# Putting the experts' sums back to the tokens with rounded parts of 512 columns in place of plain float32 products

## The chip, the cores and the metric

The kernel runs on one core of a Trainium2 chip. The core has TensorE (matrix products into the accumulator banks, PSUM), VectorE, ScalarE, GpSimd, and a sync engine (SyncE) that issues the large transfers from device memory; 16 DMA engines carry them. The engines run apart and wait for one another only by semaphores. The metric is the time of one execution on the device in microseconds, the median of several runs. All numbers are float32; a "rounded" tile (float32r in the trace) is a float32 tile that TensorE reads in a shortened form, in one pass instead of several.

## What is computed

The reference runs one block of four sublayers and then a second block of two layers over 256 tokens of 1024 channels. The change lies in the last sublayer of the first block, a mixture of eight experts with two chosen per token:

```python
def moe_ffn(h, router, w_gu, w_down):
    logits = (h @ router).astype(jnp.float32)
    top_val, top_idx = lax.top_k(logits, TOP_K)
    weights = jax.nn.softmax(top_val, axis=-1)
    gate = jnp.sum(jax.nn.one_hot(top_idx, N_EXPERTS, dtype=jnp.float32) * weights[..., None], axis=-2)
    out = jnp.zeros(h.shape, jnp.float32)
    for e in range(N_EXPERTS):
        out = out + gate[..., e:e + 1] * swiglu(h, w_gu[e], w_down[e])
    return out
```

With `swiglu(h, w_gu, w_down)` the product of silu(g) * u with `w_down`, where g and u are the two halves of `h @ w_gu`. Each expert is 1024 x 7168 and 3584 x 1024, 44 MB of weights.

## The kernel before

**One expert at a time, for the tokens it has.** The kernel first works out which tokens each expert takes (up to 128 fit in one round; a second round, called `again`, runs only if some expert has more, and is skipped here by a branch on a flag (`second`, L2755, with the test at L190 and the skipped side's semaphore counts at L195)). For an expert x a one-hot matrix `Pe` (tokens by places) gathers its tokens by a product into `XGf` and its rounded parts `XGh`, `XGl`. Then 14 weight tiles of 512 columns give seven pairs of rows (`hrow`), which are turned and split into `hTh`, `hTl`, and 28 row blocks of the second matrix give the sum of 128 places by 1024 channels in two accumulator banks.

**Products in three parts.** To keep float32 accuracy, every weight and every activation is split into a rounded high part and the rest: high times high, high times low and low times high are accumulated. Weights arrive in slots of 2 MB (three of them, `slots`), and each slot is used in two *units* of 128 x 2048. For every unit ScalarE copies the slot into `uh_moe_w` (rounding, `split_hi`, L362), VectorE subtracts (`ul_moe_w`, `split_lo`, L374), and TensorE does twelve products of 512 columns. An expert has 42 units, numbered l = 0 to 41 below: 0 to 27 for the first matrix, 28 to 41 for the second. High and low parts have three buffers each, so the high part of unit n waits until TensorE has used unit n-3 (L368). A slot is given back when the low part of its second unit is done (L380).

**The end of an expert and the put.** When the sum is complete, `summed_vector` (L2635) multiplies it by the sublayer's gate row into `Y`, two pieces of 512 columns (the tile shows as `HT` in the trace, since Y lies in it). `put_tensor` (L2531) then brings it back to the tokens: for each half `hf` of the tokens and each half `i` of the channels one product with `PT`, the turned one-hot matrix, as weights and a piece of Y streamed through:

```python
e.matmul(ps.t[:, :], PT[x % 2][:, hf, :], Y[:, i * 512:(i + 1) * 512])
```

`put_vector` (L2540) adds the four results, times the token's gate, to X.

**What sets the order.** Nothing is scheduled by a planner: each engine's stream is written by the loops `round_tensor`, `round_scalar` and `round_vector` (L2649 to L2678). ScalarE and VectorE run two units ahead: at step n they split unit n and then do `use_scalar` or `use_vector` of unit n-2. So on VectorE the sums of expert x (`use_vector`, l = 41) stand behind the low part of unit 1 of expert x+1 and ahead of that of unit 2. On TensorE the put of expert x stands behind unit 3 of expert x+1, in the middle of its weight products. For the last expert it stands at the end: the sums, the put, the additions, and then the norm that begins on ScalarE (`norm_scalar`, L526, after a table load, L142). On VectorE the last sums and the additions stand behind the branch (`last_put`, L2829); on ScalarE the branch comes after the last unit's high part. The second block's first layer starts with memsets on GpSimd, which wait for TensorE's count behind its own branch, and then the first splits (`uh_in`, `ul_in`).

Of the kernel before, what the change touches and what calls it, by code (L numbers as in the profile page):

```python
# [6 lines left out]
F32 = mybir.dt.float32  # L7
R32 = mybir.dt.float32r
AF = mybir.ActivationFunctionType
AX = mybir.AxisListType  # L10

D = 1024
# [11 lines left out]
NE = 8  # L24
# [1008 lines left out]
def hybrid(c):  # L1033
# [586 lines left out]
    def branch_tensor(e, br):  # L1620
# [3 lines left out]
        for hf in range(2):  # L1624
# [22 lines left out]
            e.wait_ge(*ps.was)  # L1647
            e.wait_ge(*v.at(("PT", br, hf)))
            e.wait_ge(*a.at(("PT", br, hf)))
# [729 lines left out]
def experts(c):  # L2379
# [5 lines left out]
    M = c.moe = Stage(c, "moe")  # L2385
    again = c.again = Stage(c, "again")
    HT = c.put(98.5, "HT3", [128, KC, T])
    ph = c.above(114.5)
    PT = [c.sb(f"PTe{i}", [128, 2, 128], ph) for i in range(2)]
    rw = c.sb("rw", [128, KC, NE], ph)  # L2390
    L, gt = c.sb("L", [128, 2, NE], ph), c.sb("egate", [128, 2, NE], ph)
    sel, pos = c.sb("esel", [128, 2, NE], ph), c.sb("epos", [128, 2, NE], ph)
# [5 lines left out]
    hTh, hTl = c.put(40.5, "ehTh", [128, 28, 128], R32), c.put(54.5, "ehTl", [128, 28, 128], R32)  # L2398
    XGh, XGl = c.put(106.5, "XGh", [128, KC, 128], R32), c.put(110.5, "XGl", [128, KC, 128], R32)
    XGf, Y = HT[:, 0:4, :].rearrange("p a (b s) -> p (a b) s", s=128), HT[:, 4:8, :].rearrange("p a b -> p (a b)")  # L2400
    Pe = c.put(68.5, "Pe", [128, 2, 128])
    hrow = [c.put(70.5 + 2 * i, f"hrow{i}", [128, 512]) for i in range(2)]
    router_landed, norm_landed, raw_landed = c.event_signal("router_landed", 16), c.event_signal("final_norm_landed", 16), c.event_signal("raw_landed", 16)
# [21 lines left out]
    NU, PER = len(U), 42  # L2425
    dbanks, ubanks = c.pool(range(6, 8)), c.pool(range(6))

    def at(n):

        return n // PER, n % PER  # L2430
# [35 lines left out]
    def gather_vector(e, S, blk, x, step):  # L2466
        if step == 0:
            e.wait_ge(*M.v.at("pos"))
            if x:
                e.wait_ge(*S.t.at(("XG", x - 1, 4)))  # L2470
            for hf in range(2):
                e.tensor_scalar(Pe[:, hf, :], K["iota"][:, blk * CAP:blk * CAP + 128], pos[:, hf, x:x + 1], ALU.is_equal, sel[:, hf, x:x + 1], ALU.mult).then_inc(*S.v.up(("Pe", x)))
        if step == 2:
            ps = c.psum.of((S.name, "PT", x))
            e.wait_ge(*S.t.at(("PT", x)))
            if x > 1:
                e.wait_ge(*S.t.at(("put", x - 2)))
            e.tensor_copy(PT[x % 2][:, :, :].rearrange("p h t -> p (h t)"), ps.t[:, 0:256]).then_inc(*S.v.up(("PT", x)))
            c.psum.leave((S.name, "PT", x), S.v)
        if step in (3, 4):  # L2480
            k0 = 4 * (step - 3)
            ps = c.psum.of((S.name, "XG", x, k0))
            e.wait_ge(*S.t.at(("XG", x, k0)))
            if x:
                e.wait_ge(*S.v.at(("XGl", x - 1, 4)))
            else:
                e.wait_ge(*M.t.at("logits"))
            for k in range(k0, k0 + 4):
                e.tensor_scalar(XGf[:, k, :], ps.t[:, (k - k0) * 128:(k - k0 + 1) * 128], s1[:, k:k + 1], ALU.mult, s2[:, k:k + 1], ALU.add).then_inc(*S.v.up(("XGf", x, k0)))
            c.psum.leave((S.name, "XG", x, k0), S.v)  # L2490
        if step == 5:
            for k0 in (0, 4):
                e.wait_ge(*S.a.at(("XGh", x, k0)))
                e.tensor_tensor(XGl[:, k0:k0 + 4, :], XGf[:, k0:k0 + 4, :], XGh[:, k0:k0 + 4, :].bitcast(F32), ALU.subtract).then_inc(*S.v.up(("XGl", x, k0)))
# [19 lines left out]
    def hidden_scalar(e, S, x, j):  # L2514
        ps = c.psum.of((S.name, "hT", x, j))
        e.wait_ge(*S.t.at(("hT", x, j)))
        if x:
            e.wait_ge(*S.t.at(("Y", x - 1, 1)))
        elif S is M:
            e.wait_ge(*S.v.at(("w", "lo", 7)))  # L2520
        e.activation(hTh[:, 4 * j:4 * j + 4, :].rearrange("p a s -> p (a s)"), ps.t[:, :], AF.Copy).then_inc(*S.a.up(("hTh", x, j)))
# [9 lines left out]
    def put_tensor(e, S, x):  # L2531
        for hf in range(2):
            for i in range(2):
                ps = ubanks.take((S.name, "put", x, hf, i))
                e.wait_ge(*ps.was)
                e.wait_ge(*S.v.at(("Y", x, i)))
                e.matmul(ps.t[:, :], PT[x % 2][:, hf, :], Y[:, i * 512:(i + 1) * 512]).then_inc(*S.t.up(("put", x, hf, i)))
        S.t.mark(("put", x))

    def put_vector(e, S, x):  # L2540
        e.wait_ge(*M.v.at("gate"))
        for hf in range(2):
            for i in range(2):
                o = X[:, hf, i * 512:(i + 1) * 512]
                ps = c.psum.of((S.name, "put", x, hf, i))
                e.wait_ge(*S.t.at(("put", x, hf, i)))
                if x:
                    e.wait_ge(*S.v.at(("X", x - 1)))
                e.scalar_tensor_tensor(o, ps.t[:, :], gt[:, hf, x:x + 1], o, ALU.mult, ALU.add).then_inc(*S.v.up(("X", x)))
                c.psum.leave((S.name, "put", x, hf, i), S.v)  # L2550
            if x == NE - 1:
                S.v.mark(("X_half", hf))
# [44 lines left out]
    def use_scalar(e, S, n):  # L2597
        x, l = at(n)
        if l < 28:
            j = l // 4  # L2600
            if l % 4 == 1 and j:
                hidden_scalar(e, S, x, j - 1)
            if l % 4 == 3:
                ps = c.psum.of((S.name, "row", x, j, 0))
                e.wait_ge(*S.t.at(("row", x, j, 0)))
                if j > 1:
                    e.wait_ge(*S.t.at(("hT", x, j - 2)))
                elif x:
                    e.wait_ge(*S.t.at(("hT", x - 1, 6 - j % 2)))
                e.activation(hrow[j % 2][:, :], ps.t[:, :], AF.Silu).then_inc(*S.a.up(("silu", x, j)))  # L2610
                c.psum.leave((S.name, "row", x, j, 0), S.a)
        elif l == 28:
            hidden_scalar(e, S, x, 6)

    def use_vector(e, S, n):
        x, l = at(n)
        if l < 28:
            j = l // 4
            if l % 4 == 1 and j:
                hidden_vector(e, S, x, j - 1)  # L2620
            if l % 4 == 3:
                ps = c.psum.of((S.name, "row", x, j, 1))
                e.wait_ge(*S.t.at(("row", x, j, 1)))
                e.wait_ge(*S.a.at(("silu", x, j)))
                e.tensor_tensor(hrow[j % 2][:, :], hrow[j % 2][:, :], ps.t[:, :], ALU.mult).then_inc(*S.v.up(("h", x, j)))
                c.psum.leave((S.name, "row", x, j, 1), S.v)
            if l == 3 and x:
                put_vector(e, S, x - 1)
            return
        if l == 28:  # L2630
            hidden_vector(e, S, x, 6)
        if l == PER - 1 and (x < NE - 1 or S is again):
            summed_vector(e, S, x)

    def summed_vector(e, S, x):  # L2635
        e.wait_ge(*c.side.v.at(("gate", "moe")))
        e.wait_ge(*(S.t.at(("put", x - 1)) if x else M.t.at("logits")))
        for i in range(2):
            ps = c.psum.of((S.name, "Y", x, i))
            e.wait_ge(*S.t.at(("Y", x, i)))  # L2640
            e.tensor_tensor(Y[:, i * 512:(i + 1) * 512], ps.t[:, :], g[:, i * 512:(i + 1) * 512], ALU.mult).then_inc(*S.v.up(("Y", x, i)))
            c.psum.leave((S.name, "Y", x, i), S.v)
# [26 lines left out]
    def round_vector(e, S, W, blk, begun):  # L2669
        for n in range(NU + AHEAD):  # L2670
            if (EARLY if S is M else 0) <= n < NU:
                W.split_lo(e, n)
            if n == AHEAD - 1:
                begun(e)
            if n >= AHEAD:
                use_vector(e, S, n - AHEAD)
                if coming(n - AHEAD):
                    gather_vector(e, S, blk, *coming(n - AHEAD))  # L2678
# [143 lines left out]
    def vector(e):  # L2822
        norm_vector(c, e, M, 1)
        before.wait_for(e, "end")
        turned_half(e, M, M.v, True)
        round_vector(e, M, U, 0, routed_vector)
        begun = M.v.n

        def last_put():  # L2829
            M.v.n = begun  # L2830
            summed_vector(e, M, NE - 1)
            put_vector(e, M, NE - 1)
            M.v.mark("end")

        with second(e, [again.v], last_put):
            last_put()
            M.wait_for(e, "end")
            round_vector(e, again, U2, 1, lambda e: [gather_vector(e, again, 1, 0, s) for s in range(6)])
            put_vector(e, again, NE - 1)
        again.v.mark("end")  # L2840
        e.wait_ge(*norm_landed.at("norm"))
        for h in range(2):
            e.wait_ge(*again.a.at(("rst", h)))
            e.scalar_tensor_tensor(X[:, h, :], X[:, h, :], c.rst[:, h:h + 1], fn[:, :], ALU.mult, ALU.mult).then_inc(*again.v.up(("X", h)))
# [1001 lines left out]
```

## Time and profile before

| | |
|---|---|
| Median of 3 runs | 2587.92 us (2586.27 to 2588.69) |
| The profiled execution | 2586.29 us, of which the trace spans 2584.5 us |
| TensorE products, share of the span | 93% |
| VectorE | 77% |
| ScalarE | 55% |
| Experts, first weight unit to the last addition into X | about 749 to 1749 us |
| Bytes moved | 613 MB, mean 237 GB/s |

Busy time is the time in which an engine had an instruction in work. For TensorE a record's end is modelled: a product is shown for 0.39 us even where the next one starts 0.23 us after it, so the spacing of starts, not the mean duration, is the price of a product in a dense stream. The granted clock is the share of TensorE's full clock that the chip let it have (1.00 is 2.4 GHz, 0.50 is 1.2 GHz). "Idle before" is the time for which the engine had nothing in work ahead of an instruction, with the instruction of another engine that released it. A window's row gives its bounds and length, the busy us (and instructions) of TensorE, its weight loads, VectorE, ScalarE and GpSimd, then the granted clock, the DMA share and GB/s; some windows below are of TensorE alone.

### The profile page before, as it was taken

The page shows a single profiled execution, that of the slowest core. Times are in us where ns is not written, and L with a number is a line of the kernel's source. Part 1 is how long each engine was busy: PE and PEld are TensorE (multiplying, and loading weights), DVE is VectorE, ACT ScalarE, POOL GpSimd, SP SyncE. Part 2 cuts the span into 40 slices and gives each one's busy share as a digit, 9 for nine tenths or more (in the row PEclk, how much of TensorE's full clock was granted, in tenths as well). Part 3 has the DMA queues.
Part 4 walks back from the last instruction along what each step waited for, and adds up shares of the span by engine and source line. Part 5 has one row for each costly group of instructions (what it writes and reads, how often), then busy time and mean ns, then how long its engine had stood idle before and what let it go on. Part 6 is the DMA issues. An engine that isn't in the chain of part 4 may idle for free.

```text
span 2584.5 us, 32676 instructions
## 1 busy us (share of the span) xinstructions
PE 2391.6 (93%) x13786; PEld 2081.0 (81%) x13786; DVE 1981.9 (77%) x2136; ACT 1426.6 (55%) x1578; POOL 221.0 (9%) x274
## 2 busy tenths in 40 slices
PE   4877799899989999999999999997998998997998
PEld 3756699698868888888888888886987997886996
DVE  6656777689769898988988888886666766666675
ACT  3311444367647676767777777764354553434562
POOL 1101011001000000000000000002301110311110
PEclk9986899999989999999999999999998998998999
DMA  9662577644449999999999999984224554213551
GB/s 321 209 217 90 195 275 279 214 156 163 171 171 362 341 368 339 368 338 360 348 360 347 344 362 348 360 296 177 99 82 147 180 196 147 99 66 134 192 194 68
DMA packets 264741, 612.64 MB, mean 237 GB/s; under 512 B 18616, under 2 KB 33227, under 8 KB 264587
## 3 DMA queue, kind: packets, MB, share of 16 engines
q1 hardware_dynamic: 247808, 554.39, 59.7%
q0 software_dynamic: 15824, 55.72, 6.4%
q8 instruction: 110, 1.80, 0.3%
q10 hardware_dynamic: 954, 0.37, 0.1%
q14 instruction: 45, 0.36, 0.0%
HBM read 609.37 MB, written 1.08 MB: 236 GB/s over the span
## 4 chain that ended last, share of the span: by engine, by line
PE 79%; DVE 12%; ACT 4%; DMA 2%; issue 2%; POOL 1%; SPq 0%; PEldq 0%; PEld 0%; DVEq 0%; ACTq 0%; POOLq 0%
PE ps L132 77%; PE ps L136 2%; DVE eb L145 1%; DVE gate L153 1%; DMA slots<-in_hyb_mod_w 1%; DVE ul_ssm_w L145 1%; DVE X L153 1%; DVE ul_in L145 1%; DVE xn L153 1%; DVE macc L153 1%; DMA beside<-in_dense_mod_w 1%; ACT uh_ffn L139 1%; DVE gcv L153 0%; DVE xn L145 0%; ACT xn L139 0%
## 5 line engine op out<-in xcount | busy, mean ns | idle before, releaser
L145 DVE TENSOR_TENSOR ul_moe_w<-slots,uh_moe_w 128x2048 fp32r<-128x2048 f32 x334 | 762.7, 2290 | 108.0 <-ACT uh_moe_w L139 107.9
L139 ACT ACTIVATE uh_moe_w<-slots 128x2048 fp32r<-128x2048 f32 x334 | 640.3, 1918 | 215.5 <-PE ps L132 195.0
L132 PE MATMUL ps<-uh_moe_w,XGh 128*128 128x512 f32 x896 | 356.4, 398 | 3.1 <-DVE XGl L145 2.1
L132 PE MATMUL ps<-uh_moe_w,XGl 128*128 128x512 f32 x896 | 349.5, 390 | 0.0
L132 PE MATMUL ps<-ul_moe_w,XGh 128*128 128x512 f32 x896 | 349.0, 389 | 0.0
L145 DVE TENSOR_TENSOR ul_ffn<-slots,uh_ffn 128x2048 fp32r<-128x2048 f32 x62 | 142.1, 2292 | 101.0 <-ACT uh_ffn L139 101.0
L132 PE MATMUL ps<-HTf,uh_ffn 128*128 128x256 f32 x704 | 201.4, 286 | 2.8 <-DVE HTlf L145 2.8
L132 PE MATMUL ps<-HTlf,uh_ffn 128*128 128x256 f32 x704 | 201.0, 285 | 0.0
L132 PE MATMUL ps<-HTf,ul_ffn 128*128 128x256 f32 x704 | 200.8, 285 | 0.0
L132 PEld LDWEIGHTS ps<-uh_moe_w,XGh 128*128 128x128 f32 x896 | 168.3, 188 | 38.5 <-DVE XGl L145 2.2
L132 PEld LDWEIGHTS ps<-uh_moe_w,XGl 128*128 128x128 f32 x896 | 168.2, 188 | 35.7
L132 PEld LDWEIGHTS ps<-ul_moe_w,XGh 128*128 128x128 f32 x896 | 168.5, 188 | 35.2 <-issue 1.7
L139 ACT ACTIVATE uh_ffn<-slots 128x2048 fp32r<-128x2048 f32 x66 | 125.7, 1911 | 96.4 <-PE ps L132 96.4
L132 PE MATMUL ps<-uh_moe_w,ehTh 128*128 128x512 f32 x448 | 177.2, 396 | 0.0
L132 PE MATMUL ps<-ul_moe_w,ehTh 128*128 128x512 f32 x448 | 174.6, 390 | 0.0
L132 PEld LDWEIGHTS ps<-HTf,uh_ffn 128*128 128x128 f32 x704 | 137.0, 195 | 3.6 <-DVE HTlf L145 3.6
L132 PE MATMUL ps<-uh_moe_w,ehTl 128*128 128x512 f32 x448 | 138.1, 389 | 0.0
L132 PEld LDWEIGHTS ps<-HTlf,uh_ffn 128*128 128x128 f32 x704 | 137.1, 195 | 0.0
L132 PEld LDWEIGHTS ps<-HTf,ul_ffn 128*128 128x128 f32 x704 | 137.0, 195 | 0.0
L145 DVE TENSOR_TENSOR ul_dense_w<-slots,uh_dense_w 128x2048 fp32r<-128x2048 f32 x33 | 75.5, 2291 | 44.6 <-ACT uh_dense_w L139 44.6
L132 PE MATMUL ps<-HTm,uh_in 128*128 128x256 f32 (+1 forms) x336 | 102.3, 305 | 6.9 <-DVE HTlm L145 3.9
L139 ACT ACTIVATE uh_dense_w<-slots 128x2048 fp32r<-128x2048 f32 x33 | 62.9, 1912 | 77.3 <-PE ps L132 77.2
(512 smaller groups left out, 5508.4 us busy)
## 6 DMA issues: line engine op xcount, KB each, us to landing
slots<-in_moe_w_gu SPq DMA_DIRECT2D x111, 2048.0 KB, 8.8
slots<-in_moe_w_down SPq DMA_DIRECT2D x56, 2048.0 KB, 8.0
slots<-in_w_up SPq DMA_DIRECT2D x20, 2048.0 KB, 8.0
slots<-in_w_in SPq DMA_DIRECT2D x14, 2048.0 KB, 8.7
slots<-in_dense_w_gu SPq DMA_DIRECT2D x10, 2048.0 KB, 10.3
slots<-in_ssm_w_in SPq DMA_DIRECT2D x10, 2048.0 KB, 8.4
slots<-in_w_down SPq DMA_DIRECT2D x10, 2048.0 KB, 8.4
slots<-in_dense_w_down SPq DMA_DIRECT2D x5, 2048.0 KB, 11.7
```

The lines of the kernel that those rows point to most:

```text
L132: return self.e.matmul(o, lhsT, rhs, start=start, stop=stop, skip_group_check=skip) if self.e else DONE
L136: return self.e.transpose(o, i, ident[0:n, 0:n]) if self.e else DONE
L139: return self.e.activation(o, i, f, **kw) if self.e else DONE
L145: return self.e.tensor_tensor(o, a, b, op) if self.e else DONE
L153: return self.e.scalar_tensor_tensor(o, a, s, b, op0, op1) if self.e else DONE
```

## The change

`PT` becomes a rounded tile (its entries are 0 and 1). Two new tiles `Yh` and `Yl` of 128 x 1024 (`eYh`, `eYl` in the trace) hold the high part and the rest of Y. ScalarE writes Yh in `use_scalar` at the last unit of an expert (l = 41), VectorE writes Yl in a new function `low_sum_vector`, called in `use_vector` at unit 0 of the next expert, and for the last expert between the sums and the additions. Each put product becomes two that accumulate.

```diff
-    PT = [c.sb(f"PTe{i}", [128, 2, 128], ph) for i in range(2)]
+    PT = [c.sb(f"PTe{i}", [128, 2, 128], ph, R32) for i in range(2)]
...
+    Yh, Yl = c.put(120, "eYh", [128, D], R32), c.put(102.5, "eYl", [128, D], R32)
...
             for i in range(2):
                 ps = ubanks.take((S.name, "put", x, hf, i))
                 e.wait_ge(*ps.was)
-                e.wait_ge(*S.v.at(("Y", x, i)))
-                e.matmul(ps.t[:, :], PT[x % 2][:, hf, :], Y[:, i * 512:(i + 1) * 512]).then_inc(*S.t.up(("put", x, hf, i)))
+                e.wait_ge(*S.v.at(("PT", x)))
+                e.wait_ge(*S.a.at(("Yh", x, i)))
+                cs = slice(i * 512, (i + 1) * 512)
+                e.matmul(ps.t[:, :], PT[x % 2][:, hf, :], Yh[:, cs], True, False)
+                e.wait_ge(*S.v.at(("Yl", x, i)))
+                e.matmul(ps.t[:, :], PT[x % 2][:, hf, :], Yl[:, cs], False, True).then_inc(*S.t.up(("put", x, hf, i)))
...
         elif l == 28:
             hidden_scalar(e, S, x, 6)
+        elif l == PER - 1:
+            for i in range(2):
+                cs = slice(i * 512, (i + 1) * 512)
+                e.wait_ge(*S.v.at(("Y", x, i)))
+                e.activation(Yh[:, cs], Y[:, cs], AF.Copy).then_inc(*S.a.up(("Yh", x, i)))
+
+    def low_sum_vector(e, S, x):
+        for i in range(2):
+            cs = slice(i * 512, (i + 1) * 512)
+            e.wait_ge(*S.a.at(("Yh", x, i)))
+            e.tensor_tensor(Yl[:, cs], Y[:, cs], Yh[:, cs].bitcast(F32), ALU.subtract).then_inc(*S.v.up(("Yl", x, i)))
 
     def use_vector(e, S, n):
         x, l = at(n)
+        if l == 0 and x:
+            low_sum_vector(e, S, x - 1)
...
             summed_vector(e, M, NE - 1)
+            low_sum_vector(e, M, NE - 1)
             put_vector(e, M, NE - 1)
```

The order of instructions on the engines, at the seam between expert 0 and expert 1 (the same at every seam). First ScalarE, with the semaphores each row waits for; `moe_tensor` counts TensorE's uses, `moe_vector` VectorE's results, `weights..._landed` the slots. Before:

```order
475 L139 ACTIVATE uh_moe_w<-slots 128x2048 [waits moe_tensor]
476 L139 ACTIVATE uh_moe_w<-slots 128x2048 [waits moe_tensor,weights1_landed]
477 L139 ACTIVATE uh_moe_w<-slots 128x2048 [waits moe_tensor]
478 L139 ACTIVATE uh_moe_w<-slots 128x2048 [waits moe_tensor,weights2_landed]
479 L139 ACTIVATE uh_moe_w<-slots 128x2048 [waits moe_tensor]
480 L139 ACTIVATE uh_moe_w<-slots 128x2048 [waits moe_tensor,weights0_landed]
481 L139 ACTIVATE uh_moe_w<-slots 128x2048 [waits moe_tensor]
482 L139 ACTIVATE hrow<-ps 128x512
```

And the same stretch of ScalarE with the change:

```order
475 L139 ACTIVATE uh_moe_w<-slots 128x2048 [waits moe_tensor]
476 L139 ACTIVATE uh_moe_w<-slots 128x2048 [waits moe_tensor,weights1_landed]
477 L139 ACTIVATE uh_moe_w<-slots 128x2048 [waits moe_tensor]
478 L139 ACTIVATE eYh<-HT 128x512 [waits moe_vector] x2
479 L139 ACTIVATE uh_moe_w<-slots 128x2048 [waits moe_tensor,weights2_landed]
480 L139 ACTIVATE uh_moe_w<-slots 128x2048 [waits moe_tensor]
481 L139 ACTIVATE uh_moe_w<-slots 128x2048 [waits moe_tensor,weights0_landed]
482 L139 ACTIVATE uh_moe_w<-slots 128x2048 [waits moe_tensor]
483 L139 ACTIVATE hrow<-ps 128x512
```

Rows 476 and 477 are units 0 and 1 of the new expert; the two copies of Y now stand between unit 1 and unit 2 and wait for VectorE.

On VectorE, the same seam, after the change against before (the `HT` row is the scaling of the sums into Y):

```order
 L145 TENSOR_TENSOR ul_moe_w<-slots,uh_moe_w 128x2048 x7
 L145 TENSOR_TENSOR HT<-ps,gate 128x512 x2
-L145 TENSOR_TENSOR ul_moe_w<-slots,uh_moe_w 128x2048 x4
+L145 TENSOR_TENSOR ul_moe_w<-slots,uh_moe_w 128x2048
+L145 TENSOR_TENSOR eYl<-HT,eYh 128x512 x2
+L145 TENSOR_TENSOR ul_moe_w<-slots,uh_moe_w 128x2048 x3
 L145 TENSOR_TENSOR hrow<-hrow,ps 128x512
 L153 SCALAR_TENSOR_TENSOR X<-ps,egate,X 128x512 x4
```

The two subtractions for Yl stand behind the low part of unit 2 and ahead of that of unit 3.

On TensorE, the put behind unit 3, after the change against before:

```order
 L132 MATMUL ps<-uh_moe_w,XGl 128x512
-L132 MATMUL ps<-HT,PTe 128x512 x4
+L132 MATMUL ps<-eYh,PTe 128x512
+L132 MATMUL ps<-eYl,PTe 128x512
+L132 MATMUL ps<-eYh,PTe 128x512
+L132 MATMUL ps<-eYl,PTe 128x512
+L132 MATMUL ps<-eYh,PTe 128x512
+L132 MATMUL ps<-eYl,PTe 128x512
+L132 MATMUL ps<-eYh,PTe 128x512
+L132 MATMUL ps<-eYl,PTe 128x512
 L132 MATMUL ps<-uh_moe_w,XGh 128x512
```

The put keeps its place; four products become eight.

## Rows read from the trace of the kernel before

**Rows 1.** Window of one expert, all engines

```profile
1002.00:1124.00 122.00, 122.00 (x562) 100.04 (x561) 108.87 (x74) 86.01 (x58) 0.00 (x0) 1.00 0.96 352
```

**Rows 2.** Put products of two experts (ns min/median/max, first and last start us)

```profile
L132 PE MATMUL ps<-HT,PTe x8: 590/592/592, 1008.1 to 1011.1; 128*128 128x512 f32 x8
...
L132 PE MATMUL ps<-HT,PTe x8: 590/592/592, 1133.1 to 1136.1; 128*128 128x512 f32 x8
```

**Rows 3.** Timeline of TensorE at a seam (start us, us, instruction): unit 2, put, unit 4

```profile
1002.62 0.39 PE L132 MATMUL ps<-uh_moe_w,XGh 128*128 128x512 f32 x1
...
1008.06 3.59 PE L132 MATMUL ps<-HT,PTe 128*128 128x512 f32 x8
...
1011.72 0.40 PE L132 MATMUL ps<-ul_moe_w,XGh 128*128 128x512 f32 x1
```

**Rows 4.** Page, costliest groups: the low parts (busy, mean ns, idle before)

```profile
L145 DVE TENSOR_TENSOR ul_moe_w<-slots,uh_moe_w 128x2048 fp32r<-128x2048 f32 x334 | 762.7, 2290 | 108.0 <-ACT uh_moe_w L139 107.9
```

**Rows 5.** Timeline of VectorE at the same seam

```profile
998.82 1.28 DVE L145 TENSOR_TENSOR HT<-ps,gate 128x512 f32<-128x512 f32 x2
1000.02 4.48 DVE L145 TENSOR_TENSOR ul_moe_w<-slots,uh_moe_w 128x2048 fp32r<-128x2048 f32 x2
...
1009.70 0.68 DVE L145 TENSOR_TENSOR hrow<-hrow,ps 128x512 f32<-128x512 f32 x1
1010.30 2.72 DVE L153 SCALAR_TENSOR_TENSOR X<-ps,egate,X 128x512 f32<-128x512 f32 x4
```

**Rows 6.** Timeline of ScalarE at the same seam: units 2, 4 and 6

```profile
997.44 1.92 ACT L139 ACTIVATE uh_moe_w<-slots 128x2048 fp32r<-128x2048 f32 x1 [0.86 <-PE ps L132]
...
1003.30 1.92 ACT L139 ACTIVATE uh_moe_w<-slots 128x2048 fp32r<-128x2048 f32 x1 [1.28 <-DMA slots<-in_moe_w_gu]
...
1008.93 1.91 ACT L139 ACTIVATE uh_moe_w<-slots 128x2048 fp32r<-128x2048 f32 x1 [1.00 <-DMA slots<-in_moe_w_gu]
```

**Rows 7.** Timeline, pairs of 128x512 on ScalarE and on VectorE

```profile
977.45 1.13 ACT L139 ACTIVATE XGh<-HT 128x512 fp32r<-128x512 f32 x2
...
979.78 1.28 DVE L145 TENSOR_TENSOR XGl<-HT,XGh 128x512 fp32r<-128x512 f32 x2
```

**Rows 8.** Page, DMA issues: KB each, median us to landing

```profile
slots<-in_moe_w_gu SPq DMA_DIRECT2D x111, 2048.0 KB, 8.8
```

**Rows 9.** Timeline of TensorE: two products after an idle gap

```profile
631.63 0.70 PE L132 MATMUL ps<-msq,ones 128*128 128x256 f32 x2 [2.20 <-ACT msq L139]
...
749.11 0.50 PE L132 MATMUL ps<-uh_moe_w,XGh 128*128 128x512 f32 x1 [2.06 <-DVE XGl L145]
```

**Rows 10.** Windows behind these gaps (length, TensorE busy, granted clock, DMA share, GB/s)

```profile
632.00:634.00 2.00, 2.00 (x13) 0.64 0.00 0
634.00:636.00 2.00, 2.00 (x11) 0.50 0.00 0
...
750.00:752.00 2.00, 2.00 (x11) 1.00 0.03 8
```

**Rows 11.** Timeline from the last sums to the next layer

```profile
1743.42 1.29 DVE L145 TENSOR_TENSOR HT<-ps,gate 128x512 f32<-128x512 f32 x2 [3.69 <-PE ps L132]
...
1741.25 1.28 ACT L142 ACT_TABLE_LOAD   x1 [3.85 <-DVEq L195]
1746.97 1.06 ACT L139 ACTIVATE xn<-X 128x1024 f32<-128x1024 f32 x1 [4.44 <-DVE X L153]
...
1751.87 0.52 POOL L174 MEMSET uh_in<- 128x512 f32 x1 [1030.48 <-PEq L195]
...
1754.28 1.23 DVE L145 TENSOR_TENSOR ul_in<-slots,uh_in 128x1024 fp32r<-128x1024 f32 x1 [0.26 <-ACT uh_in L139]
```

**Rows 12.** Sequencers at the branch (ns min/median/max, start us)

```profile
L190 ACTq TENSOR_LOAD <-fli x1: 467/467/467, 1735.5 to 1735.5; - x1
L190 PEldq COMPARE_BRANCH x1: 5978/5978/5978, 1745.6 to 1745.6; - x1
...
L195 ACTq EVENT_SEMAPHORE  x1: 17/17/17, 1738.7 to 1738.7; - x1
```

More of the change, by code:

```diff
@@ L2838, in vector @@
             round_vector(e, again, U2, 1, lambda e: [gather_vector(e, again, 1, 0, s) for s in range(6)])
+            low_sum_vector(e, again, NE - 1)
             put_vector(e, again, NE - 1)
```

## The prediction

> **What bounds the kernel now.** I read the page by stage first. The experts run from about 750 to 1748 us; expert by expert the windows repeat: in the 122 us of one of them TensorE is busy throughout, at a granted clock of 1.00, VectorE for 109, ScalarE for 86, with the DMA share at 0.96 [rows 1]. So TensorE sets the pace, if its products really lie end to end. The put products of two experts begin 125.0 us apart [rows 2], and between them nothing waits on TensorE: 24 products of 512 columns take 1008.06 - 1002.62 = 5.44 us, 0.227 us each, 2.72 us for one weight unit (12 products) [rows 3]. What is taken off TensorE here comes off the time, and whatever makes it wait is added.
>
> Next, how near the other engines are. A unit n goes round a ring: TensorE finishes n-3, ScalarE rounds n into the high part, VectorE subtracts the low part (2.29 us) [rows 4], TensorE uses n. At the seam between two experts VectorE also scales the two sums (1.28 us) before the low part of unit 2 of the new expert, which it does from 1000.02 to 1002.31 [rows 5]. TensorE starts unit 2 at 1002.62. The slack is 0.3 us. ScalarE (1.92 us a unit) begins its part of unit 2 at 997.44, early [rows 6]. This is the place on which the change lands.
>
> **What it removes.** A plain product of 512 columns is two records in the trace, 0.59 us each as modelled, eight for an expert's four products [rows 2]. Their real price is the spacing: 1008.06 to the second product of unit 4 at 1011.72 is 3.66, less one ordinary step 0.23, so 3.43 us for eight records [rows 3]. The new form is eight products with rounded operands, 512 columns, at the 0.227 us of the unit products: 1.81 us. Saved: 1.61 us per put; seven of the eight puts lie inside the dense stream, so 11.3 us in all, if nothing waits. The Trainium skill, "TensorE: Matmul & The Clock Gate", section "Back-to-back issue gap", gives about 131 ns as the sustained spacing of load and product pairs at 512 columns. By that the eight would take 1.05 us and the saving be 2.4 us per put; this stream of such pairs shows 227 ns [rows 3], and I go by the row.
>
> **What it adds at a seam, step by step** (times of the seam in [rows 3], [rows 5], [rows 6]; the step of one engine to the next costs some 0.05 us).
> ScalarE ends the high part of unit 1 at 996.58 (997.44 less its idle 0.86). Before, it goes straight on to unit 2. Now the two copies of Y stand there, and they wait for VectorE's scaled sums, done at 999.46 and 1000.10. Everything queued behind them on ScalarE waits as well, unit 2 first. A pair of copies of 128x512 takes ScalarE 1.13 us and a pair of such subtractions VectorE 1.28 [rows 7]; two copies that each wait I count at 0.6. So the copies run 999.5 to 1000.1 and 1000.15 to 1000.7; the high part of unit 2 runs 1000.7 to 1002.6, in place of 997.44 to 999.36; the low part 1002.65 to 1004.95, in place of 1000.02 to 1002.31. TensorE starts unit 2 at 1005.0, in place of 1002.62: **a stall of 2.35 us**.
> Then VectorE does the two new subtractions, 1004.9 to 1006.1, and the low part of unit 3 only after them: to 1008.35. TensorE has finished unit 2 at 1007.7 and waits again: **0.65 us**. Unit 3 ends at 1011.07, the put (its low parts long ready) at 1012.88, where before it ended at 1011.48. Late by 1.40 us = 2.35 + 0.65 - 1.61.
> Does it get worse after? High part of unit 5 waits for unit 2 and runs 1007.9 to 1009.8, its low part 1010.45 to 1012.7; then the product with the silu (0.68), four additions into X (2.72) [rows 5], low part of unit 6 to 1018.2, and TensorE comes to unit 6 at 1018.8. Slack 0.6, so no third stall. The DMA: before, ScalarE waits for a landing at 1003.30 and 1008.93 [rows 6]; now it comes to those two units at 1004.4 and 1011.3, later than both landings. The slot of units 8 and 9 is given back at 1008.35 and needed at 1019.4, 11 us, while a transfer takes 8.8 us from issue to landing [rows 8]. So no new wait for DMA.
> Seven seams: **+9.8 us**. The copy of PT into a rounded tile keeps its size; I take it at nothing.
>
> **The clock.** A stall of 2.35 us between issues is 2.2 us of idle as the trace counts it (the modelled end of a product lies 0.16 us behind the next issue). Row by row such gaps go both ways: after an idle of 2.20 at 631.63 the granted clock fell to the 1.2 GHz level for about 3.4 us (0.64 of a 2 us window, then 0.50); after 2.06 at 749.11 it stayed at 1.00 [rows 9, 10]. A fall takes half of 3.4 us, 1.7 us, but the slower unit 2 then covers the second wait of 0.65, so 1.05 net. The stall lies between the two rows; I take two falls in seven seams, **+2.1 us**, and keep 0 and 7 as ends (0 to 12 us, the last with nothing covered). The Trainium skill, same page, "Why this matters for your kernels", lets the clock fall only for idle gaps longer than this stall; by it this term is 0 and the forecast 2.1 us lower. The first of the two rows speaks against it.
>
> **The last put** is in series: sums scaled from 1743.42, put, additions, norm [rows 11]. The rounded parts put ScalarE and VectorE (0.6 us each) ahead of the first product and TensorE gets 1.6 us back; VectorE's four additions end at about the same time. But ScalarE now copies Y (second copy from 1744.75) before it tests the flag. Its test took from 1735.5 to 1738.7 [rows 12], 3.2 us, and lay in idle time; now it ends at 1747.95, the table load (1.28) at 1749.25, and the norm, at 1746.97 before, starts 2.3 us late. X is then finished at about 1754.0. What covers that: TensorE's own branch of 5978 ns, from 1745.6, holds the memset on GpSimd to 1751.87, and VectorE's first sizeable work of the next layer to 1754.28 [rows 11, 12]. Cover by 0.3 us, so I take +0.1; if it is gone, up to +2.3; if TensorE's branch ends earlier, -0.5.
>
> **Sum**: 9.8 + 2.1 + 0.1 = 12.0 us. The profiled execution took 2586.3 (span 2584.5), 1.6 below the median of the runs, 2587.9; it becomes 2598.3, and the median 2599.9.
>
> **Rivals.**
> 1. The clock falls at nearly every seam: 9.8 + 7 x 1.05 = +17.2, 2605; with nothing covered +21.7, 2610. For it: the 2.20 of [rows 9]. Against: the 2.06.
> 2. The gain stays (the other side). Mechanism: TensorE has a unit more in hand at the seam than I read, so that ScalarE's wait for Y is hidden; then 7 x 1.61 comes off: 2576. It decides at a wait of ScalarE that ends 0.3 us later than now. Against it: slack of 0.3 us against 2.65 us of delay, at a seam that repeats [rows 2].
> 3. It cancels: the two stalls together are 1.0 to 2.3 us, because the copies are issued earlier or a landing that I take as on time was the limit before. 2583 to 2593, say 2588.
> 4. The rounded products don't do what they say and cost what a record of the plain form costs, 0.43 us. Nothing saved, 7 x 3.0 = +21, 2609. Against: 0.227 for the same form in [rows 3].
>
> **Chances.** Forecast (two stalls, up to four falls, 2592 to 2603): 0.66. Rival 1: 0.14. Rival 2: 0.06. Rival 3: 0.10. Rival 4: 0.04. Range 2592 to 2611: takes in the forecast, rivals 1 and 4, and leaves out about 0.16. 0.2% is 5.2 us, about what a measurement of this kernel can tell from no change: faster 0.06, same 0.11 (rival 3 and a little of the forecast's lower end), slower 0.83.
>
> **What would show it.** ScalarE's copies of Y stand with idle time of about 2.9 us ahead of them, released by VectorE's sums; seven waits of TensorE for a low part of unit 2, about 2.2 us of idle, each followed by one of about 0.5; put products at 0.227 us; puts of two experts 126.4 us apart, 127.5 where the clock fell. It is wrong if TensorE doesn't wait at the seam (rival 2), if the put's eight products take 3.4 us (rival 4), or if X of the last put holds the next layer.

## The result and the profile after

The changed kernel is **slower by 0.6%**: 2604.94 us, the median of 6 runs (2598.03 to 2606.57), beside 2587.69 us for the kernel before (6 runs on the same chip, 2586.27 to 2592.85). The ratio is 1.0060, with a 95% interval of 1.0046 to 1.0075, or 15.5 us with 11.9 to 19.4. The forecast was 2599.9 us, +12.0. The profiled execution took 2606.04 us with a span of 2604.2 us; before it was 2586.3 and 2584.5.

First the seam between two experts, TensorE's timeline of the kernel after (start us, us, instruction, in brackets the idle time before it and what ended it). It answers to [rows 3].

```profile
1006.79 0.39 PE L132 MATMUL ps<-uh_moe_w,XGl 128*128 128x512 f32 x1
1009.34 0.50 PE L132 MATMUL ps<-uh_moe_w,XGh 128*128 128x512 f32 x1 [2.17 <-DVE ul_moe_w L145]
1009.68 0.40 PE L132 MATMUL ps<-ul_moe_w,XGh 128*128 128x512 f32 x1
...
1011.99 0.39 PE L132 MATMUL ps<-uh_moe_w,XGl 128*128 128x512 f32 x1
1012.75 0.50 PE L132 MATMUL ps<-uh_moe_w,XGh 128*128 128x512 f32 x1 [0.37 <-DVE ul_moe_w L145]
...
1015.60 0.39 PE L132 MATMUL ps<-eYh,PTe 128*128 128x512 f32 x1
1015.83 0.39 PE L132 MATMUL ps<-eYl,PTe 128*128 128x512 f32 x1
```

There are two waits where before there was none: 2.17 us of idle before unit 2, 0.37 before unit 3, both ended by VectorE's low part. The put's products follow at steps of 0.23 us, as the unit products do. Now VectorE and ScalarE at the same seam, which answer to [rows 5] and [rows 6].

```profile
1003.21 1.28 DVE L145 TENSOR_TENSOR HT<-ps,gate 128x512 f32<-128x512 f32 x2
1007.00 2.29 DVE L145 TENSOR_TENSOR ul_moe_w<-slots,uh_moe_w 128x2048 fp32r<-128x2048 f32 x1 [2.51 <-ACT uh_moe_w L139]
1009.21 1.28 DVE L145 TENSOR_TENSOR eYl<-HT,eYh 128x512 fp32r<-128x512 f32 x2
1010.41 6.69 DVE L145 TENSOR_TENSOR ul_moe_w<-slots,uh_moe_w 128x2048 fp32r<-128x2048 f32 x3
```

```profile
1003.93 1.23 ACT L139 ACTIVATE eYh<-HT 128x512 fp32r<-128x512 f32 x2 [2.96 <-DVE HT L145]
1005.06 5.50 ACT L139 ACTIVATE uh_moe_w<-slots 128x2048 fp32r<-128x2048 f32 x3
1012.42 1.92 ACT L139 ACTIVATE uh_moe_w<-slots 128x2048 fp32r<-128x2048 f32 x1 [1.85 <-PE ps L132]
```

They are to be read as one chain. ScalarE stands idle for 2.96 us because the next instruction in its queue is the copy of a sum that VectorE has not scaled yet. Then it copies, then it rounds unit 2 (from 1005.06). VectorE in turn is idle for 2.51 us, released by ScalarE, and gives TensorE the low part of unit 2 at 1009.29. Its two new subtractions stand between that and the low part of unit 3, which makes the second wait.

The waits of the whole stretch 760 to 1760 us (engine and line, released by what: us in total, times, longest us):

```profile
ACT eYh L139 <- DVE HT L145: 27.4, 8, 6.7
PEld ps L132 <- DVE ul_moe_w L145: 23.5, 13, 2.6
PE ps L132 <- DVE ul_moe_w L145: 18.0, 13, 2.2
```

So 13 waits of TensorE: one at the start of the experts, which is there before as well, seven before a unit 2, five before a unit 3. The two seams without the second wait are those where the clock fell. One of them in TensorE's timeline, and the clock around both (window, its length, TensorE's busy time with the number of records, granted clock, DMA share, GB/s), to be held against [rows 9, 10]:

```profile
1263.46 0.80 PE L132 MATMUL ps<-uh_moe_w,XGh 128*128 128x512 f32 x1 [2.17 <-DVE ul_moe_w L145]
1264.05 0.63 PE L132 MATMUL ps<-ul_moe_w,XGh 128*128 128x512 f32 x1
...
1266.98 0.39 PE L132 MATMUL ps<-uh_moe_w,XGl 128*128 128x512 f32 x1
```

```profile
1135.00:1140.00 5.00, 4.09 (x12) 0.72 0.56 205
1140.00:1145.00 5.00, 5.00 (x22) 0.94 0.91 320
1145.00:1150.00 5.00, 5.00 (x24) 1.00 1.03 373
1255.00:1260.00 5.00, 5.00 (x24) 1.00 1.04 383
1260.00:1265.00 5.00, 2.83 (x10) 0.85 1.03 380
1265.00:1270.00 5.00, 5.00 (x20) 0.81 0.45 134
```

The steps between products are 0.43 us (1264.05 to 1264.48 and on) where they are else 0.23: the lower of the two levels, 1.2 GHz, for about 3.4 us. Full speed less the granted clock is 0.28 and 0.06 of 5 us at the first fall and 0.15 and 0.19 of 5 us at the second: 1.7 us each, half of the 3.4.

Last, the end of the experts, which answers to [rows 11, 12]: timeline of all engines, then the sequencers' records (ns min/median/max, first and last start us).

```profile
1758.77 1.29 DVE L145 TENSOR_TENSOR HT<-ps,gate 128x512 f32<-128x512 f32 x2 [3.50 <-PE ps L132]
1759.50 1.23 ACT L139 ACTIVATE eYh<-HT 128x512 fp32r<-128x512 f32 x2 [6.74 <-DVE HT L145]
...
1766.13 1.28 ACT L142 ACT_TABLE_LOAD   x1 [5.41 <-issue]
1767.43 1.06 ACT L139 ACTIVATE xn<-X 128x1024 f32<-128x1024 f32 x1
...
1768.87 0.52 POOL L174 MEMSET uh_in<- 128x512 f32 x1 [1044.68 <-PEq L195]
...
1775.78 0.43 PE L132 MATMUL ps<-HTm,uh_in 128*36 128x256 f32 x1 [1.46 <-DVE HTlm L145]
```

```profile
L190 ACTq COMPARE_BRANCH  x1: 50/50/50, 1760.8 to 1760.8; - x1
...
L190 PEldq COMPARE_BRANCH  x1: 6242/6242/6242, 1762.4 to 1762.4; - x1
L195 ACTq EVENT_SEMAPHORE  x1: 17/17/17, 1766.1 to 1766.1; - x1
```

ScalarE tests the flag only after its copies, and its jump takes from 1760.9, where the compare ends, to 1766.1. The table load stands behind the jump, so the norm begins only at 1767.43.

**Where the time went**, by marks in the two traces (us):

| stretch | before | after | difference |
|---|---|---|---|
| start to the first product of the first unit | 749.11 | 751.93 | +2.8 |
| from there to the scaling of the last sums | 994.31 | 1006.84 | +12.5 |
| scaling of the last sums to the next layer's first product | 14.54 | 17.01 | +2.5 |
| the rest | 826.54 | 828.42 | +1.9 |

The first and the last stretch run the same code in both kernels. The mark of the first lies between 747.97 and 752.69 in the nine other traces of this study, and the rest took 824.2 to 828.7 us in them, so these 4.7 us are no more than single executions differ by. The two others, 15.0 us, are the change; the ratio of the runs gives 15.5.

### The profile page after: what moved, and what is told of

It is laid out like the page before. It is cut to its first block, busy times and chain, and to the rows that moved or that the text cites. A ratio compares the mean times of both kernels' runs of the same rounds, so it can differ in the third digit from the quotient of the medians.

```text
span 2604.2 us, 32708 instructions
## 1 busy us (share of the span) xinstructions
PE 2393.8 (92%) x13786; PEld 2089.5 (80%) x13786; DVE 1990.7 (76%) x2152; ACT 1434.7 (55%) x1594; POOL 221.0 (8%) x274
## 4 chain that ended last, share of the span: by engine, by line
PE 76%; DVE 14%; ACT 6%; DMA 2%; issue 2%; POOL 1%; SPq 0%; ACTq 0%; DVEq 0%; POOLq 0%
PE ps L132 74%; PE ps L136 2%; DVE ul_moe_w L145 2%; ACT uh_moe_w L139 1%; DVE eb L145 1%; DVE gate L153 1%; DMA slots<-in_hyb_mod_w 1%; DVE ul_ssm_w L145 1%; DVE X L153 1%; DVE ul_in L145 1%; DVE xn L153 1%; ACT uh_ffn L139 0%; DVE macc L153 0%; ACT xn L139 0%; DVE gcv L153 0%
## 6 DMA issues: line engine op xcount, KB each, us to landing
slots<-in_dense_w_down SPq DMA_DIRECT2D x5, 2048.0 KB, 11.6
```

## The experiments

The theory by then: the loss is ScalarE's queue. The copies wait for VectorE's sums with the rounding of unit 2 behind them, and VectorE's subtractions stand ahead of the low part of unit 3; the cheap put itself is a gain of 1.6 us a seam. Rivals: the mere load of the added copies and subtractions, with the engines near their limit at the seam; or products that are not cheaper than they look. A third question was the end of the experts. Changes are against the kernel after unless said.

| kernel | median us | before, same chip | ratio (95%) | put to put, us |
|---|---|---|---|---|
| the change | 2604.94 | 2587.69 | 1.0060 (1.0046 to 1.0075) | 126.55; with a fall 127.5 |
| e1 products alone | 2577.25 | 2589.61 | 0.9951 (0.9935 to 0.9968) | 123.40 to 123.51; one 125.08 |
| e2 copies alone | 2615.87 | 2589.61 | 1.0104 (1.0087 to 1.0121) | 128.22; with a fall 129.1 |
| e3 both late | 2578.12 | 2589.61 | 0.9954 (0.9937 to 0.9970) | 123.35 to 124.46 |
| e4 both late, last put plain | 2577.21 | 2589.61 | 0.9953 (0.9936 to 0.9970) | 123.36 to 124.36 |
| e5 subtractions late | 2598.22 | 2586.61 | 1.0038 (1.0023 to 1.0052) | 125.94; with a fall 127.55 |
| e6 last put plain | 2599.18 | 2586.61 | 1.0037 (1.0022 to 1.0051) | 126.56; with a fall 127.5 |
| e7 copies in the middle | 2581.52 | 2586.61 | 0.9976 (0.9966 to 0.9985) | 123.98 |
| e8 next loads held | 2607.25 (1 run) | | | 126.6; with a fall 127.5 |

Before, the puts are 125.04 us apart.

**e1, the products alone.** The scaled sum goes rounded into Yh and is put twice; nothing is copied or subtracted. The kernel leaves out the low part, so its X is another one and only its time is used.

```
     def put_tensor(e, S, x):
-                e.wait_ge(*S.a.at(("Yh", x, i)))
+                e.wait_ge(*S.v.at(("Y", x, i)))
...
-                e.matmul(ps.t[:, :], PT[x % 2][:, hf, :], Yl[:, cs], False, True)
+                e.matmul(ps.t[:, :], PT[x % 2][:, hf, :], Yh[:, cs], False, True)
...
-            e.tensor_tensor(Y[:, i * 512:(i + 1) * 512], ps.t[:, :], g[:, i * 512:(i + 1) * 512], ALU.mult)
+            e.tensor_tensor(Yh[:, i * 512:(i + 1) * 512], ps.t[:, :], g[:, i * 512:(i + 1) * 512], ALU.mult)
```

> The products alone: the scaled sums are written rounded and each put streams them twice (eight products of 512 columns, rounded operands), with no copy on ScalarE and no subtraction on VectorE; the low part is left out, so X is another one. Theory (TensorE is the bound, and the loss of the change comes from where the copies stand): 1.61 us less at each of seven seams, no wait of TensorE at units 2 and 3, puts of two experts 123.4 us apart, about 2576 us, 11 to 12 under the kernel before. Rival (the rounded products bring nothing in this stream, or TensorE isn't the bound there): 2588, no change.

Measured: 0.9951, 12.4 us faster by the medians. A seam in TensorE's timeline of this kernel:

```profile
1009.07 1.98 PE L132 MATMUL ps<-eYh,PTe 128*128 128x512 f32 x8
1010.88 0.39 PE L132 MATMUL ps<-uh_moe_w,XGh 128*128 128x512 f32 x1
```

Eight products in 1010.88 - 1009.07 = 1.81 us, to the hundredth what the sum had taken. 125.04 - 123.45 = 1.6 us per seam. The saving is real, and it is not the products that cost. The one seam of 125.08 has late weights: ScalarE waits 3.21 us for a landing, and TensorE then 1.25 us for a low part.

**e2, the copies alone.** Copies and subtractions where the change has them, into tiles that nobody reads; the put takes Y by the plain product.

```
+    Yh, Yl = c.put(120, "eYh", [128, D], R32), c.put(124, "eYl", [128, D], R32)
...
-                e.matmul(ps.t[:, :], PT[x % 2][:, hf, :], Yh[:, cs], True, False)
-                e.matmul(ps.t[:, :], PT[x % 2][:, hf, :], Yl[:, cs], False, True)
+                e.matmul(ps.t[:, :], PT[x % 2][:, hf, :].bitcast(F32), Y[:, i * 512:(i + 1) * 512])
```

> The copies alone: ScalarE's copies of Y and VectorE's subtractions stand where the change puts them (the low part goes to a tile of its own), but the put is the plain float32 product of Y, and what they write is not read. Theory (a copy that waits for Y ahead of unit 2, a subtraction ahead of unit 3): TensorE idle 2.17 us before unit 2 and about 0.35 before unit 3 at each seam, 2.7 us late each, 19 us over seven, 1.0 for each fall of the clock (two to five of them), and 2 us more at the end because ScalarE tests the flag late: 2609 to 2614 us. Rival (the added work fits into idle time of ScalarE and VectorE, and the loss comes from the new products): 2588.

Measured: 1.0104, 26.3 us slower by the medians; 2615.87 us lies 2 us above the range expected. A seam without a fall of the clock is 128.22 - 125.04 = 3.2 us longer, and the idle times are those of the change (TensorE's timeline of this kernel):

```profile
1398.30 0.50 PE L132 MATMUL ps<-uh_moe_w,XGh 128*128 128x512 f32 x1 [2.17 <-DVE ul_moe_w L145]
1401.70 0.50 PE L132 MATMUL ps<-uh_moe_w,XGh 128*128 128x512 f32 x1 [0.39 <-DVE ul_moe_w L145]
```

The clock fell at 5 of 7 seams, the upper end of what was expected, so it is not what lay above. That is the seam itself, 3.2 us in place of 2.7 (the slower products behind a wait, priced below, were not in the sum), and a kernel before that took 2589.61 us on this chip, where the sum started from 2588. The two halves add up: 3.2 - 1.6 = 1.6 us a seam, the change has 1.5. But e2 doesn't tell the place in the queue from the load. e3 does.

**e3, the same work later.** The copies stand after the high part of unit 3 of the next expert, the subtractions after its low part.

```
+def high_sum_scalar(e, S, x):
+    for i in range(2):
+        cs = slice(i * 512, (i + 1) * 512)
+        e.wait_ge(*S.v.at(("Y", x, i)))
+        e.activation(Yh[:, cs], Y[:, cs], AF.Copy).then_inc(*S.a.up(("Yh", x, i)))
...
+        if l == 1 and x:
+            high_sum_scalar(e, S, x - 1)
...
-        elif l == PER - 1:
+        elif l == PER - 1 and x == NE - 1:
+            high_sum_scalar(e, S, x)
...
     def use_vector(e, S, n):
-        if l == 0 and x:
+        if l == 1 and x:
             low_sum_vector(e, S, x - 1)
```

> The change with the same work at another place: ScalarE copies Y after the high part of unit 3 of the next expert (not of unit 1), VectorE subtracts after the low part of unit 3 (not of unit 2); the last expert stays as in the change. Theory (head of the line blocking): the sums are long ready when ScalarE comes to the copies, no idle of TensorE at units 2 and 3, at most 0.2 us at unit 6, so 1.4 to 1.6 us less than before at each seam; the end still costs 2 us or so: 2578 to 2580 us, faster than both. Rival (the added 1.2 us on ScalarE and 1.3 us on VectorE cost at a seam wherever they stand, since VectorE has only 10% idle): 2595 to 2605.

Measured: 0.9954, 11.5 us **faster than before** by the medians, with every instruction of the change in place. ScalarE's timeline at a seam of this kernel:

```profile
999.82 1.93 ACT L139 ACTIVATE uh_moe_w<-slots 128x2048 fp32r<-128x2048 f32 x1 [0.74 <-PE ps L132]
1001.65 1.14 ACT L139 ACTIVATE eYh<-HT 128x512 fp32r<-128x512 f32 x2
1002.93 1.93 ACT L139 ACTIVATE uh_moe_w<-slots 128x2048 fp32r<-128x2048 f32 x1 [0.15 <-DMA slots<-in_moe_w_gu]
```

The copies wait for nothing and take 1.14 us; TensorE does not wait at unit 2 or 3 of any seam. The clean seams of e3 are 123.35 to 123.42 us long, those of e1, without copies and subtractions, 123.40 to 123.51. So load is not the cause: 1.14 us more on ScalarE and 1.28 on VectorE are free where the weights are on time, and the place in the queue costs the 3.1 us. What is left between 123.42 and 124.46 goes with landings that now come late. At the longest seam ScalarE waits 1.69 and 1.21 us for weights and TensorE 0.76 us for a low part; whether the added work makes such a wait longer is not shown. ScalarE's waits for weights grew from 18 (20.5 us) before to 27 (24.5 us), this way (waits of e3 from 760 to 1735 us):

```profile
ACT uh_moe_w L139 <- DMA slots<-in_moe_w_gu: 21.0, 23, 1.7
...
ACT uh_moe_w L139 <- DMA slots<-in_moe_w_down: 3.5, 4, 1.0
PE ps L132 <- DVE ul_moe_w L145: 2.1, 3, 1.0
```

**e4, e3 with the last put plain** and so with no copies ahead of the flag test. Against e3:

```
     def put_tensor(e, S, x):
+                if x == NE - 1:
+                    e.wait_ge(*S.v.at(("Y", x, i)))
+                    e.matmul(ps.t[:, :], PT[x % 2][:, hf, :].bitcast(F32), Y[:, i * 512:(i + 1) * 512])
+                    continue
...
-        elif l == PER - 1 and x == NE - 1:
-            high_sum_scalar(e, S, x)
...
         def last_put():
-            low_sum_vector(e, M, NE - 1)
```

> As the run before, and the put of the last expert is the plain product of Y, without copies, as in the kernel before. Theory: the end is as in the kernel before, since ScalarE tests its flag at the old place; 1.5 to 2.7 us less than the run before, 2576 to 2578 us, and the test on ScalarE takes 3.2 us again in place of 6.0. Rival (the end was hidden after all, and the 2.7 us by which the transposes of X came later in the changed kernel were given back within the next layer): no difference to the run before.

Measured: 0.9953. By the medians 0.9 us below e3, which is less than the runs can tell apart. By the traces the stretch from the last sums to the next layer's first product is 14.49 us beside 16.84 in e3 (14.54 before), so the end is as the theory has it, but the time of the whole does not show it (expected were 1.5 to 2.7 us less). e3 and e4 are the best versions found, and both beat both kernels.

**e5, the subtractions alone late** (the copies stay where the change has them).

```
     def use_vector(e, S, n):
-        if l == 0 and x:
+        if l == 1 and x:
             low_sum_vector(e, S, x - 1)
```

> The change with one part moved: VectorE's subtraction for the low sums after the low part of unit 3 (not of unit 2); ScalarE's copies stay ahead of unit 2. Theory (two stalls with two causes): the idle of 2.17 us before unit 2 stays at each seam, the one of 0.35 before unit 3 goes, puts 125.9 to 126.1 us apart where the clock doesn't fall (126.55 in the change); 0.5 us a seam, 3.5 us less than the change, about 2601. The clock may still fall, since it is the long idle that brings that. Rival (the second wait comes from the late high part of unit 3, not from the subtraction): no difference to the change, 2605.

Measured: 1.0038. The puts are 125.94 apart, 0.6 less than in the change; the wait before unit 3 is gone at every seam, the one before unit 2 stays (2.17 to 2.44). That is the second wait by itself: 0.6 us a seam. The median lies 11.6 us above the kernel before, where the change lies 17.3 above; seven seams account for 4.3 of these 5.7 us and one fall of the clock less for some of the rest.

**e6, the change with its last put plain**: e4's branch in `put_tensor` on the kernel after, and

```
-        elif l == PER - 1:
+        elif l == PER - 1 and x < NE - 1:
...
         def last_put():
-            low_sum_vector(e, M, NE - 1)
```

> The change with the put of the last expert as a plain product of Y, without copies. Theory: from the scaling of the last sums to the first product of the next layer 14.5 us as in the kernel before, where the change has 17.0; 2.5 us less than the change, about 2602; seams unchanged (126.55 us, or 127.5 with a fall of the clock). Rival (the next layer gives it back): 2605.

Measured: 1.0037. Last sums to next layer 14.69 us beside 17.01 in the change: the 2.3 us at the end come from there. The seams are as in the change. The median lies 12.6 us above the kernel before, 4.7 less than the change does, which is more than the end explains; the two intervals overlap, so the 2.3 us rest on the traces and not on the times of the whole.

**e7, the copies one place later only**: after the high part of unit 2, the subtractions as in the change.

```
+        if l == 0 and x:
+            high_sum_scalar(e, S, x - 1)
...
-        elif l == PER - 1:
+        elif l == PER - 1 and x == NE - 1:
+            high_sum_scalar(e, S, x)
```

> ScalarE's copies after the high part of unit 2, VectorE's subtraction where the change has it, after the low part of unit 2 and ahead of that of unit 3; the last expert as in the change. Theory: no idle at unit 2, but the low part of unit 3 comes 1.3 us later and TensorE is idle for 0.3 to 0.5 us before unit 3 at each seam; too short for a fall of the clock; puts 123.9 to 124.1 us apart; 7 us less over the seams, 2.5 more at the end: about 2583. Rival (only ScalarE's wait costs, the subtraction is free): as with both moved behind unit 3, puts 123.4 apart, 2578.

Measured: 0.9976, over 10 runs (2579.44 to 2585.61). One step in ScalarE's queue turns a loss of 0.6% into a gain of 0.24%. The timelines of ScalarE, VectorE and TensorE of this kernel show the rest of the price:

```profile
998.43 1.92 ACT L139 ACTIVATE uh_moe_w<-slots 128x2048 fp32r<-128x2048 f32 x1 [0.86 <-PE ps L132]
1000.53 1.23 ACT L139 ACTIVATE eYh<-HT 128x512 fp32r<-128x512 f32 x2 [0.18 <-DVE HT L145]
```

```profile
1003.21 1.28 DVE L145 TENSOR_TENSOR eYl<-HT,eYh 128x512 fp32r<-128x512 f32 x2
1004.41 4.49 DVE L145 TENSOR_TENSOR ul_moe_w<-slots,uh_moe_w 128x2048 fp32r<-128x2048 f32 x2
```

```profile
1006.75 0.50 PE L132 MATMUL ps<-uh_moe_w,XGh 128*128 128x512 f32 x1 [0.26 <-DVE ul_moe_w L145]
1007.09 0.39 PE L132 MATMUL ps<-ul_moe_w,XGh 128*128 128x512 f32 x1
```

The copies still wait, but for 0.18 us. The subtractions ahead of the low part of unit 3 cost 0.26 of idle, at each of the seven seams, and 0.6 in time (123.98 less the 123.4 of a clean seam of e3): the modelled end of a product hides another 0.16 us of the wait, and the slower products behind it take the rest.

**e8, the next layer's loads held back.** In the change ScalarE's jump took 5.2 us where before it took 2.4. The 2 MB loads of the next layer's weights run just then. Here SyncE issues them only when ScalarE has passed its jump.

```
     def sync(e):
+        e.wait_ge(*again.a.at("end"))
```

> The change, with the next layer's weight loads held back until ScalarE has passed its test of the flag. Looked at in the trace alone. Theory (ScalarE's jump to the skipped side waits for its instructions, which come by the same DMA engines as the 2 MB loads of the next layer): from the jump to the count on the other side 2.4 us as in the kernel before, where the change has 5.2. Rival (the jump is long for another reason, as the copies just ahead of it): 5.2 again. The loads come 9 us later, so the next layer starts later and the time is no lower, 2605 to 2612.

Measured, in one run: the jump takes 2.7 us again (1759.7 to 1762.4), and TensorE's 3.3 us, which took 5.9 to 6.4 in all other traces. The DMA engines are all but idle over ScalarE's jump here (share 0.04) and full in the change (1.06); before, the share over the jump was 0.01. Sequencers' records of e8:

```profile
L190 ACTq COMPARE_BRANCH  x1: 50/50/50, 1759.7 to 1759.7; - x1
...
L190 PEldq COMPARE_BRANCH  x1: 3342/3342/3342, 1761.3 to 1761.3; - x1
L195 ACTq EVENT_SEMAPHORE  x1: 17/17/17, 1762.4 to 1762.4; - x1
```

The whole is not faster, 2607.25, since the weights now come late: the next layer's first product stands 20.2 us after the last sums in place of 17.0. As a version it is no use; it shows that the loads lengthen the jump.

## Why the prediction was right, and where it was off

The direction and the mechanism at the seams were right; one step, the end, was mis-sized, and one small term was missing. The median lies 5.0 us above the forecast and inside its range. Step by step:

- **The saving of the put: right.** 1.61 us were taken, 1.81 us for eight products is what the traces show, and e1 gives 1.6 a seam. Rival 4 falls. The choice of the row over the page was right too: the Trainium skill, "TensorE: Matmul & The Clock Gate", section "Back-to-back issue gap", gives about 131 ns for such pairs; the trace does not agree, the steps of these 512-column products are 0.227 us.
- **The first wait: right.** Forecast a stall of 2.35 us, 2.2 as idle; measured 2.17 of idle, and 1009.34 - 1006.79 less one step of 0.23 is 2.32. ScalarE's idle of 2.96 was forecast as about 2.9. Rival 2, that ScalarE's wait stays hidden, falls, since 2.6 us of delay stood against 0.3 of slack. So does rival 3: the two stalls are 2.85 us together, not 1.0 to 2.3. e7 shows the same bound from the other side: with ScalarE's order changed by one place the wait of TensorE is gone.
- **The second wait: right in kind, 0.1 too large.** Forecast 0.65; measured 1012.75 - 1011.99 - 0.23 = 0.53. The low part of unit 3 ends 3.36 us after unit 2 began (1010.41 + 2.29 against 1009.34), 3.35 in the forecast; but unit 2 itself took 0.15 longer than 2.72, which covered part of the wait.
- **A term that was missing: the restart**, the slower products just behind a wait. The first product after each wait takes a step of 0.34 in place of 0.23, and the few behind it are slightly slow: 2.65 us for the 11 steps of unit 2 from 1009.34 to 1011.99 where 2.50 is ordinary, 2.85 for the 12 of unit 3 where 2.72 is. That is 0.28 a seam. So 2.32 + 0.53 + 0.28 - 1.61 = 1.52 a seam in place of 1.40; the put-to-put times say 126.55 - 125.04 = 1.51, seven times 10.6 in place of 9.8.
- **The clock: two falls in seven, as taken**, 1.9 us in place of 2.1 (127.5 against 126.55). The count was a choice and is luck: with the same wait (2.17 us in most seams, up to 2.44) it was 5, 1, 2 and 3 in e2, e5, e6 and e8, with the change's 2 it is 13 of 35. Rival 1 (nearly every seam) is not excluded for a single execution, and the traced execution of e2 came near it.
- **The end: the step that failed.** I took ScalarE's test of the flag at the 3.2 us that it has in [rows 12], and the cover of 0.3 us from TensorE's branch; +0.1 in all, up to +2.3 without cover. In the change the test takes 6.0 us, from 1760.1 to 1766.1, of which 5.2 are the jump (2.4 before). The norm starts 8.66 us after the scaling of the last sums began (1767.43 - 1758.77), 3.55 before (1746.97 - 1743.42): 5.1 late in place of the 2.3 forecast, the difference being the jump. Less the cover of 2.3 + 0.3 = 2.6 us that the prediction gave to TensorE's branch, that is the +2.5 measured, and X holds the next layer, which the prediction had named as a sign of being wrong. Moving the test put it next to the loads of the next layer's weights, and with these held back (e8) the jump takes 2.7. The cost of the jump had been read from a row where the DMA engines were idle. e6, with the test back in its old place, has 2.3 us of it back.
- **The sum.** 10.6 + 1.9 + 2.5 = 15.0 in place of 12.0. The medians are 17.3 apart. The other 2 us are not placed: single executions differ by more than that in the stretches that the change doesn't touch, and the number of falls, at 1 us each, was seen in one execution of the change alone.

The Trainium skill, "TensorE: Matmul & The Clock Gate", section "Why this matters for your kernels", warns of a throttled clock only for idle gaps longer than those seen here. The traces do not agree: the clock fell in 13 of the 35 seams that have a wait of 2.17 us or a little more, and behind the 2.20 us of [rows 9]. The length alone does not decide: it stayed up behind the longest of these waits (2.44 us, in e5). At the seams of the kernels without this wait (before, e1, e3, e4, e7) it never fell.

What stays open is which of these waits make the clock fall: I found nothing in the timelines ahead of a wait that tells the two kinds apart. Open is also whether e4 is faster than e3.

## What to carry to other kernels

When an engine's work is made cheaper by a preparation on other engines, look where the preparation stands in their queues, not what it takes: here 1.1 us on ScalarE and 1.3 on VectorE were free when put where their input was ready, and cost 3.1 us of TensorE's time when the copies stood two units and the subtractions one unit earlier, all because an instruction that must wait holds back everything behind it. Put such a step behind the work that the busiest engine needs next, as long as its own result is not yet due. A branch or a test that is moved must be priced for the traffic at its new place.

## What the runs showed of the hardware

- **A jump takes longer while large loads run.** ScalarE's jump took 2.4 to 2.7 us where it stood before the next layer's loads (before, e1, e4, e6) or with these held back (e8), and 5.0 to 5.4 us with 2 MB loads in flight (the change, e2, e3, e5, e7). TensorE's took 5.9 to 6.4 with the loads, 3.3 without. The case without loads at the later place is one execution, e8. That the code of the jump's target comes by the same DMA engines would explain it; the profile shows two packets of the instruction queues between 1760 and 1769 us of the change, but not that they were delayed.
- **A restart costs.** The first 512-column product after an idle time of 0.26 us or of 2.17 us alike has a record of 0.50 us in place of 0.39 and a step of 0.34 in place of 0.23; with what follows it some 0.13 to 0.15 us.
- **The transfers are near.** With 1.6 us taken off each expert (e1, e3, e4) the DMA share between the first put and the seventh is 0.98 where it was 0.97, and ScalarE's waits for landings in e4 are 42 with 41.8 us in place of 18 with 20.5. TensorE itself waits behind late weights only here and there, 1.25 us once in e1 and 0.28 and 0.76 in e3. That a further cut on TensorE would bring less than it takes away is what I expect; no run here tried it.
